# Final normalisation of the first block moved into the projection that opens the second block

## The reference

```python
def rmsnorm(x, g):
    y = x * rsqrt(mean(x * x, axis=-1) + EPS)
    return y * g

# first block, last lines
x = x + g2 * ec_moe(h2, router_w, exp_w1, exp_w3, exp_w2)   # 16 experts, 128 tokens each
return rmsnorm(x, final_g)                                  # input x of the second block

# second block, layer 0, first lines
h  = rmsnorm(x,   norm_g) * (1 + scale)   + shift           # 1024 tokens
hc = rmsnorm(ctx, norm_g) * (1 + scale_c) + shift_c         # 256 context tokens
p, pc = h @ w_in, hc @ w_in                                 # v, q, k, a|b, gates: 3072 columns
...
x = x + gate * mixer_out(...)                               # needs the normalised x again
```

## Time and profile before

| | us |
|---|---|
| median of 3 runs | 4442.1 (4436.2 to 4445.48) |
| the profiled execution | 4435.2 |
| its span, first to last instruction | 4433.4 |
| PE busy | 3832.5 (86%) |
| mean granted TensorE clock | 0.936 |

### The profile page before, as it was taken

The page is one execution under the profiler, slowest core; times in us unless marked ns, Lnnn a source line. Parts: engine busy times, 40 slices in busy tenths (PEclk is TensorE's granted clock), DMA queues, the critical chain, the costliest instruction groups (busy, mean ns, idle before and its releaser), DMA issues. The chain is left out here.

```text
span 4433.4 us, 44583 instructions
## 1 busy us (share of the span) xinstructions
PE 3832.5 (86%) x17507; PEld 2913.7 (66%) x17507; DVE 2574.1 (58%) x2821; ACT 1937.4 (44%) x2599; POOL 694.5 (16%) x582
## 2 busy tenths in 40 slices
PE   7899787894678789999999999499978897997988
PEld 2788643344666238787778777478867676786756
DVE  6421265327976468888888888553166525523753
ACT  4511110015545227676777776533156315423641
POOL 0200023210002101111212111320012223201222
PEclk9999898996888889999999999799989999999999
DMA  6322315101104569999999998534141234334123
GB/s 243 131 93 97 112 48 189 34 33 64 41 19 163 215 248 367 370 371 371 371 372 367 374 370 308 194 105 128 68 176 42 98 114 143 119 114 182 52 69 121
DMA packets 393094, 786.41 MB, mean 177 GB/s; under 512 B 26198, under 2 KB 109281, under 8 KB 392498
## 3 DMA queue, kind: packets, MB, share of 16 engines
q1 hardware_dynamic: 376502, 731.92, 46.1%
q0 software_dynamic: 11456, 41.16, 2.9%
q10 hardware_dynamic: 4928, 10.49, 0.7%
HBM read 671.99 MB, written 111.51 MB: 177 GB/s over the span
## 5 line engine op out<-in xcount | busy, mean ns | idle before, releaser
L2486 DVE TENSOR_TENSOR moe_w_low<-moe_w_raw,moe_w_high 128x2048 fp32r<-128x2048 f32 x384 | 882.0, 2341 | 163.7 <-ACT moe_w_high L2439 163.1
L2439 ACT ACTIVATE moe_w_high<-moe_w_raw 128x2048 fp32r<-128x2048 f32 x384 | 715.0, 1913 | 303.0 <-DMA moe_w_raw<-in_exp_w 297.0
L172 PE MATMUL moe_bank<-moe_w_high,moe_xgT_high 128*128 128x512 f32 x1024 | 404.2, 395 | 16.8 <-DVE moe_w_low L2486 12.0
L174 PE MATMUL moe_bank<-moe_w_high,moe_xgT_low 128*128 128x512 f32 x1024 | 399.6, 390 | 0.0
L173 PE MATMUL moe_bank<-moe_w_low,moe_xgT_high 128*128 128x512 f32 x1024 | 399.3, 390 | 0.0
L2758 DVE TENSOR_REDUCE layer_att_nb<-layer_att_scores 128x1 f32<-128x1280 f32 (+1 forms) x144 | 197.2, 1370 | 139.0 <-PE layer_att_scores L2664 138.9
L172 PEld LDWEIGHTS moe_bank<-moe_w_high,moe_xgT_high 128*128 128x128 f32 x1024 | 192.6, 188 | 62.8 <-DVE moe_w_low L2486 16.5
L172 PE MATMUL layer_front_bank<-layer_front_w_high,layer_front_hT_high 128*128 128x512 f32 (+1 forms) x608 | 228.8, 376 | 0.0
L174 PE MATMUL layer_front_bank<-layer_front_w_high,layer_front_hT_low 128*128 128x512 f32 (+1 forms) x608 | 222.7, 366 | 0.0
L173 PE MATMUL layer_front_bank<-layer_front_w_low,layer_front_hT_high 128*128 128x512 f32 (+1 forms) x608 | 222.4, 366 | 0.0
L174 PEld LDWEIGHTS moe_bank<-moe_w_high,moe_xgT_low 128*128 128x128 f32 x1024 | 192.6, 188 | 40.8
(11 more groups left out here) (461 smaller groups left out, 8498.3 us busy)
## 6 DMA issues: line engine op xcount, KB each, us to landing
moe_w_raw<-in_exp_w SPq DMA_DIRECT2D x192, 2048.0 KB, 10.3
mods_raw<-in_ada_w SPq DMA_DIRECT2D x12, 2048.0 KB, 9.0
h_raw<-in_w_mod SPq DMA_DIRECT2D x12, 2048.0 KB, 8.1
layer_front_raw<-in_w_in SPq DMA_DIRECT2D x48, 512.0 KB, 6.2
front_raw<-in_w_in SPq DMA_DIRECT2D x32, 512.0 KB, 6.3
proj_t<-front_out SPq DMA_DIRECT2D x48, 256.0 KB, 2.0
k_high<-layer_front_stageda SPq DMA_DIRECT2D x20, 512.0 KB, 3.3
k_low<-layer_front_stagedb SPq DMA_DIRECT2D x20, 512.0 KB, 4.7
```

Source lines behind the costliest of these rows:

```text
L172: nc.tensor.matmul(out, lhs[0], rhs[0], start=start, stop=False)
L174: return nc.tensor.matmul(out, lhs[1], rhs[0], start=False, stop=stop)
L2439: nc.scalar.activation(hi, x, ACT.Copy).then_inc(high, 1)
L2486: nc.vector.tensor_tensor(lo, x, hi.bitcast(F32), ALU.subtract).then_inc(low, 1)
```

## The change

`stage_final_norm` is gone. Its work is done inside layer0_front, as a step ahead of each tile's own normalisation: `measure_first` on ACT, `rescale` on DVE, `keep` on POOL (the store to `x2`). The two context tiles, which need none of it, come first (`order`), so the front's first loads don't depend on the experts. The weights of its group 0 and the context tiles are loaded by SP at the end of `stage_moe`, into the experts' own ring of buffers, which stays allocated; the wait for the last indirect transfer moves from POOL to SP, ahead of the load of the first token tile. In all three fronts `hT.high` is no longer computed a second time from PSUM but copied once from `whole`, as one 128 x 512 instruction on each of ACT and DVE, behind a wait for the piece before.

```diff
-def stage_front(core, name, segs, groups, rope=None):
+def stage_front(core, name, segs, order, groups, rope=None, space=None):
...
+    FIRST = NC_ if space else n
...
+        if space:
+            raw, out, x, junk, x2 = space.raw, space.out, space.x, space.junk, space.y
...
                 def load_x(t):
                     if t >= RX:
                         sp.wait_ge(turned, 2 * (t - RX) + 2)
+                    if t == FIRST:
+                        sp.wait_ge(core.scattered, 16 * E)
                     sp.dma_start(x[t % RX][:, :], tiles[t][0]).then_inc(core.load[t % RX].sem, 16)
...
+                if space:
+                    sp.dma_start(gain1, io["final_g"].partition_broadcast(P)).then_inc(gain1_loaded, 16)
...
+                if space:
+                    load_x(2)
+                    load_x(3)
...
+                def keep(t):
+                    pool.wait_ge(rescaled, t - FIRST + 1)
+                    pool.dma_start(core.x2[(t - FIRST) * P:(t - FIRST + 1) * P, :], x2[t % 2]).then_inc(core.store[t % 2].sem, 16)
+
                 for i in range(-2, N + 4):
                     if 0 <= i + 2 < n:
                         low_of(i + 2)
+                    if rescaled_tile(i + 3):
+                        keep(i + 3)
                     if R and i == 2:
                         rotation()
...
+                def measure_first(t):
+                    act.wait_ge(core.load[t % RX].sem, core.load[t % RX].at(t // RX + 1))
+                    if rescaled_tile(t - 2):
+                        act.wait_ge(core.store[t % 2].sem, kept(t - 2))
+                    core.act(act, nc.scalar.activation(x2[t % 2], x[t % RX][:, :], ACT.Square, accum_out=ss1[:, t:t + 1]))
+                    nc.scalar.activation(rms1[:, t:t + 1], ss1[:, t:t + 1], ACT.Sqrt, bias=core.eps[:, 0:1],
+                                         scale=1.0 / D).then_inc(rooted1, 1)
...
                     for k in range(4):
-                        for to in (whole[t % 2][:, k, :], hT.high[:, k, t * P:(t + 1) * P]):
-                            last = nc.scalar.activation(to, bank[4 + 2 * (t % 2)][:, k * P:(k + 1) * P], ACT.Identity,
-                                                        bias=sh[:, k:k + 1], scale=sc[:, k:k + 1])
-                    last.then_inc(out_a, 1)
+                        last = nc.scalar.activation(whole[t % 2][:, k, :], bank[4 + 2 * (t % 2)][:, k * P:(k + 1) * P],
+                                                    ACT.Identity, bias=sh[:, k:k + 1], scale=sc[:, k:k + 1])
+                    core.act(act, last)
+                    nc.scalar.activation(hT.high[:, 0:4, at], whole[t % 2][:, 0:4, :], ACT.Copy).then_inc(out_a, 1)
...
                 for i in range(-3, N + 4):
-                    if 0 <= i + 3 < n:
+                    if 0 <= i + 3 < FIRST:
                         measure(i + 3)
...
                     if 0 <= i + 2 < n:
                         modulate(i + 2)
+                    if rescaled_tile(i + 3):
+                        measure(i + 3)
+                    if rescaled_tile(i + 4):
+                        measure_first(i + 4)
...
+                def rescale(t):
+                    dve.wait_ge(rooted1, t - FIRST + 1)
+                    step(nc.vector.reciprocal(rms1[:, t:t + 1], rms1[:, t:t + 1]))
+                    if t == FIRST:
+                        dve.wait_ge(gain1_loaded, 16)
+                    nc.vector.scalar_tensor_tensor(x2[t % 2], x[t % RX][:, :], rms1[:, t:t + 1], gain1,
+                                                   ALU.mult, ALU.mult).then_inc(rescaled, 1)
...
+                    if rescaled_tile(i + 3):
+                        normalise(i + 3)
+                    if rescaled_tile(i + 4):
+                        rescale(i + 4)
...
                 for n in range(RW, E * UNITS):
                     sp.wait_ge(low, 2 * (n - RW + 1))
                     load_piece(core, sp, raw, n)
+                for j, load in enumerate(follow):
+                    sp.wait_ge(low, 2 * (E * UNITS - RW + j + 1))
+                    load(sp)
...
                 scatter(E - 1)
-                pool.wait_ge(scattered, 16 * E)
...
-def stage_final_norm(core, name="final"):
...
+    order = [(t + NT) % (NT + NC_) for t in range(NT + NC_)]
```

More of the change, by code:

```diff
@@ L618, in stage_front @@
         final[g] = i
-    assert [j[:2] for j in groups[0][1]] == [("tok", t) for t in range(n)]
+    assert [j[:2] for j in groups[0][1]] == [("tok", t) for t in order]
     plain = [i for i, (_, j) in enumerate(jobs) if j[0] != "rope"]
@@ L735, in low_of @@
                         c = slice(4 * half, 4 * half + 4)
-                        hi, lo = (v[:, c, t * P:(t + 1) * P] for v in (hT.high, hT.low))
+                        hi, lo = (v[:, c, tiles[t][3]] for v in (hT.high, hT.low))
                         nc.gpsimd.tensor_tensor(lo, whole[t % 2][:, c, :], hi.bitcast(F32), ALU.subtract).then_inc(split, 1)
@@ L947, in modulate @@
                     for k in range(4, 8):
-                        for to in (whole[t % 2][:, k, :], hT.high[:, k, t * P:(t + 1) * P]):
-                            last = nc.vector.tensor_scalar(to, bank[5 + 2 * (t % 2)][:, (k - 4) * P:(k - 3) * P],
-                                                           sc[:, k:k + 1], sh[:, k:k + 1], ALU.mult, ALU.add)
-                    last.then_inc(out_v, 1)
+                        last = nc.vector.tensor_scalar(whole[t % 2][:, k, :], bank[5 + 2 * (t % 2)][:, (k - 4) * P:(k - 3) * P],
+                                                       sc[:, k:k + 1], sh[:, k:k + 1], ALU.mult, ALU.add)
+                    step(last)
+                    nc.vector.tensor_copy(hT.high[:, 4:8, at], whole[t % 2][:, 4:8, :]).then_inc(out_v, 1)
                 def split_low(g, k):
@@ L1018, in stage_front @@
             core.hstore[RS + j].close(stores_of(j, R))
+        if space:
+            for j in range(2):
+                core.store[j].close(NT // 2)
 def stage_filter(core, name="filter"):
@@ L3273, in run_moe, with weights, context, __init__ @@
             late.close()
-        stage_moe(core, raw)
-    stage_final_norm(core)
-def run_second(core, out, l):
+        space = FrontSpace(raw, yo)
+        w = core.io["w_in_2"][0][:, 3 * BANK:4 * BANK]
+        def weights(sp):
+            for p in range(4):
+                load_front_weights(core, sp, space.raw, w, p)
+        def context(sp):
+            for t in range(NC_):
+                sp.dma_start(space.x[t], core.io["ctx_2"][0][t * P:(t + 1) * P, :]).then_inc(core.load[t].sem, 16)
+        stage_moe(core, raw, yo, (weights, context))
+        run_second_front(core, 0, space)
+class FrontSpace:
+    def __init__(self, raw, yo):
+        parts = lambda b, n: [b[:, i * (KD * BANK // n):(i + 1) * (KD * BANK // n)] for i in range(n)]
+        self.raw = raw[0][:, :].rearrange("p (k n) -> p k n", n=BANK)
+        self.x = parts(raw[1], 4)
+        self.out = parts(raw[2], 8)[0:6]
+        self.junk = parts(raw[2], 4)[3]
+        self.y = [b[:, :] for b in yo]
+def load_front_weights(core, sp, raw, w, p):
+    c = slice(2 * p, 2 * p + 2)
+    sp.dma_start(raw[:, c, :], w[2 * p * P:(2 * p + 2) * P, :].rearrange("(k p) n -> p k n", p=P)
+                 ).then_inc(core.load[4 + p].sem, 16)
+def run_second_front(core, l, space=None):
     io = core.io
@@ L3293, in run_second @@
     spans = [(0, 512), (512, 512)] + ([(SEQ, CTX)] if nctx else [])
-    groups = [(w[:, 3 * BANK:4 * BANK], [("tok", t, 0, BANK, core.v_tok[t * P:(t + 1) * P, :]) for t in range(NT + NC_)])]
+    order = [(t + NT) % (NT + NC_) for t in range(NT + NC_)]
+    groups = [(w[:, 3 * BANK:4 * BANK], [("tok", t, 0, BANK, core.v_tok[t * P:(t + 1) * P, :]) for t in order])]
     for i in range(2):
@@ L3304, in run_second @@
                         for s in range(4) for t0, n in spans]))
-    stage_front(core, name + "_front", [(x, core.sc[3 + 2 * l], m[:, 0:8, 0]), (ctx, core.sc[4 + 2 * l], m[:, 0:8, 1])],
-                groups, rope=io["qk_norm_g_2"][l])
+    segs = [(x, core.sc[3 + 2 * l], m[:, 0:8, 0], 0), (ctx, core.sc[4 + 2 * l], m[:, 0:8, 1], NT)]
+    stage_front(core, name + "_front", segs, order, groups, rope=io["qk_norm_g_2"][l], space=space)
+def run_second(core, out, l):
+    io = core.io
+    nctx = NC_ if l == 0 else 0
+    if l:
+        run_second_front(core, l)
+    x, ctx = (core.x2, io["ctx_2"][0]) if l == 0 else (core.x3, core.ctx3)
+    name = f"layer{l}"
+    tiles = range(NT + nctx)
     TL = NT + nctx
```

121 lines of the change are left out of this document (50 added, 71 removed).

## The result

The changed kernel takes 4408.5 us (median of 5 runs, 4401.08 to 4416.91), the kernel before, run beside it, 4439.25 (5 runs, 4434.14 to 4445.48): 30.75 us less, ratio 0.993 with a 95% interval of 0.9913 to 0.9947. The forecast was 4403, a gain of 38.9 us. The profiled spans differ by 4433.4 - 4404.4 = 29.0 us.

The account below looks back on a forecast made before the run. The removed stage was taken as bound by transfers and latency, the front behind it by PE. Gains of 44.1 and 1.3 us less 6.5 given back made 38.9, from 4442.1 to 4403 us; range 4394 to 4420.

Parts of the forecast that it names:

- The 69 us without PE: Between the experts' last matmul and the front's first: 69 us without PE work, which the change was to shorten.
- The meeting: Engines meeting between experts and front: forecast at 2771.7, with POOL's drain 2.66 us long and following the scatter's issue.
- the meeting still waits for the scatter: Rival: POOL's drain would not end before its transfer lands; 4.8 us less gain, 4408.0 us, chance 0.09.
- The chain on ACT: From the meeting to transposes of tile 2, ACT the longest chain: forecast 16.9 us.
- Group 0: Front's tiles 2 to 9: 6.5 us given back, PE waiting 4.8 us at tile 8 and 1.65 at tile 9.
- the first distance: Transposes of tile 2 to those of tile 3: forecast 8.04 us, PE's clock being reduced after its rest.
- the forecast's picture: Group 0: tiles 6 and 7 absorbed, PE waiting 4.8 us at tile 8 for the store behind `rotation()`.
- Copying once: High part copied once: 0.65 us saved in each of the two other fronts, 1.3 us together (0 to 2).
- 2.0 for modulate: ACT's modulate of tile 0 ahead of tile 2: four pieces of 0.345 us and one copy, 2.0 us.
- the upper bound: Cost of the high-part copy on DVE, standing behind a POOL instruction: 0.4 to 1.7 us.
- The signs named: Profile signs: no 43 us PE gap, first matmul 24 to 26 us behind, late transposes at tiles 8 and 9.
- the window: From the experts' last scatter's issue to transposes of tile 9: forecast 73.85 us, 37.6 shorter than before.

Follow-up runs that it names:

- wait_back: Changed kernel with POOL again waiting for the last scatter at the end of the experts' stage, ahead of its drain: 4407.9 us in one run.
- late_scatter: Changed kernel with the last expert's scatter issued by POOL in the next stage, after a POOL wait for `yout`: 4406.3 us, ratio 0.9928.
- best: Changed kernel with token loads one iteration earlier, `rotation()` at iteration 7, last scatter issued first in the next stage without the `yout` wait: 4399.1 us, ratio 0.9913.
- both links out: Changed kernel with token loads one iteration earlier and `rotation()` moved from iteration 2 to 7 in that front: 4404.7 us, ratio 0.9918.
- the loads sooner: Changed kernel with SP issuing each token load one iteration earlier in the second block's first front, `rotation()` unmoved: 4413.1 us in one run.
- late_rotation: Changed kernel with only `rotation()` moved on POOL from iteration 2 to iteration 7 of that front: 4406.0 us in one run.

## Why the prediction was right, and where not

**The 69 us without PE.** Right: the stretch is the one that the change works on, and the one that shrank, to 29.7 us.

**The meeting.** Wrong by 3.45 us. I took POOL's drain as a length of its own, 2.66 us, and gave the rival "the meeting still waits for the scatter" a chance of 0.09. That rival is what happens: with its own transfer under way POOL's drain took 7.89, 7.70 and 7.63 us in three profiles of the kernel; with nothing under way 2.66 and 2.58 (wait_back, late_scatter). The scatter took 6.3 us to land, so the drain ends some 1.4 us after. It doesn't wait and then drain in full: the rival's 4.8 us were 3.45. Its time, 4408.0, is nearer to the measured 4408.5 than my 4403, but half a microsecond is luck where medians of one kernel differ by several. That the row of before showed a drain "exactly behind" the landing said nothing, since the code had made POOL wait there.

**The chain on ACT.** 18.2 instead of 16.9 us. ACT's own rows came as forecast:

```profile
2777.91 1.06 ACT L834 ACTIVATE moe_w_raw<-moe_w_raw 128x1024 f32<-128x1024 f32 x1 [19.08 <-PEq L140]
2779.07 1.28 ACT L835 ACT_TABLE_LOAD   x1
2780.37 0.29 ACT L835 ACTIVATE layer_front_rms<-layer_front_ss,eps 128x1 f32<-128x1 f32 x1
2781.93 4.26 ACT L856 ACTIVATE layer_front_w_high<-moe_w_raw 128x512 fp32r<-128x512 f32 x8
2788.15 1.04 ACT L823 ACTIVATE moe_w_yo<-moe_w_raw 128x1024 f32<-128x1024 f32 x1
2792.33 1.06 ACT L834 ACTIVATE moe_w_raw<-moe_w_yo 128x1024 f32<-128x1024 f32 x1 [0.66 <-DVE moe_w_yo L992]
```

What was missed is how long DVE's instructions take beside POOL's differences. Each of these two runs beside one of POOL's L762, which start at 2789.95 and 2794.11 and take 1.26 and 1.27:

```profile
2789.98 2.31 DVE L992 SCALAR_TENSOR_TENSOR moe_w_yo<-moe_w_raw,layer_front_rms,layer_front_stageda 128x1024 f32<-128x1024 f32 x1
2794.14 1.79 DVE L999 TENSOR_SCALAR moe_w_raw<-moe_w_yo,layer_front_rstd 128x1024 f32<-128x1024 f32 x1
```

I had priced L992 at 1.29 and L999 at its median, 1.08. L992 took 2.31 and ACT stood idle for 0.66 us behind it; L999 took 0.71 more. Together that is 1.37, the missing 1.3. In late_scatter and in best, where no POOL instruction stood beside its first use, the line that answers to L992 took 1.29. The root started 0.02 us behind the table load, as before: no drain shows there.

**Group 0.** The sum came out right, 6.5 us, by luck: what makes it up was wrong. I expected tiles 6 and 7 absorbed, 4.8 us at tile 8 behind the store and 1.65 at tile 9. PE in fact waited 3.79 us at tile 7, nothing at tile 8 and 0.29 at tile 9. Of the other 2.4 us 2.1 are clock, which no step of mine had; 0.3 are small differences at tiles 7 and 9. By stretches, tiles 2 to 3, 3 to 6, 6 to 7, 7 to 8:

```profile
2796.00:2804.50 8.50, 8.50 (x33) 7.15 (x34) 6.46 (x10) 4.81 (x11) 3.54 (x4) 0.74 0.28 112
2804.50:2823.50 19.00, 19.00 (x97) 15.96 (x96) 13.21 (x26) 13.69 (x31) 12.69 (x15) 1.00 0.67 236
2823.50:2833.80 10.30, 6.52 (x33) 5.19 (x31) 6.58 (x9) 6.06 (x13) 9.83 (x11) 1.00 0.45 162
2833.80:2841.80 8.00, 8.00 (x32) 6.60 (x33) 5.64 (x10) 4.97 (x12) 3.31 (x4) 0.79 0.60 209
```

Behind the wait of 3.79 us PE is granted 0.79 on the mean of 8 us: matmuls start 0.43 us apart at first, 1.2 GHz, and 0.23 apart from 2838.17 on, 2.4 GHz. That turns 6.36 us into 8.03, 1.67 more. With both links out, where the wait at tile 7 is only 1.07 us, the clock was 1.00 in the same place and the distance 6.52. The other 0.43 is the first distance, 8.47 at a clock of 0.74 instead of 8.04 at 0.78; it differs between profiles of one kernel too (8.04 and 7.86 before, 8.47, 8.49 and 8.76 after).

Why tile 7 was late is seen on SP, ACT, POOL and DVE ahead of it:

```profile
2816.93 1.99 POOL L767 MEMSET layer_front_stagedb<- 128x1024 f32 x2
2819.80 0.47 SPq L704 DMA_DIRECT2D moe_w_raw<-x  x1
2825.56 1.06 ACT L823 ACTIVATE moe_w_yo<-moe_w_raw 128x1024 f32<-128x1024 f32 x1 [4.21 <-DMA moe_w_raw<-x]
2826.16 3.55 POOL L762 TENSOR_TENSOR layer_front_hT_low<-layer_front_whole,layer_front_hT_high 128x512 fp32r<-128x512 f32 x2
2829.65 0.63 POOL L802 DMA_DIRECT2D x<-moe_w_yo  x1
2829.86 2.00 DVE L1010 CAST layer_front_hT_high<-layer_front_whole 128x512 fp32r<-128x512 f32 x1
2831.97 1.78 DVE L999 TENSOR_SCALAR moe_w_raw<-moe_w_yo,layer_front_rstd 128x1024 f32<-128x1024 f32 x1
2833.03 1.06 ACT L823 ACTIVATE moe_w_yo<-moe_w_raw 128x1024 f32<-128x1024 f32 x1 [2.09 <-DMA x<-moe_w_yo]
```

Its load went out at 2819.80, 1.4 us later than forecast once the 7.4 us by which all of group 0 is later are taken off (2811.0 + 7.4), and took 5.8 us, not 4.0. ACT measured it at 2825.56, and on DVE the CAST of the tile before and L999 took 2.00 and 1.78 us. By my estimate that makes some 1.7 of the 3.79 us: ACT's root was ready at 2830.95, and with DVE's shortest durations L999 would have ended near 2832.0 instead of 2833.75. The store of tile 6 went out where I had put it, behind `rotation()` and `low_of(5)`, but landed 3.4 us later, not 6.2; ACT waited 2.09 us for it at tile 8, and PE didn't, since tile 7 and the clock had moved it back already. With the loads sooner the forecast's picture appears: nothing much at tile 7, 3.86 us at tile 8. So the store behind `rotation()` was a true cause, but stood behind another. The transfers from 2765 to 2865 (KB each, median us to landing), and the spread of the stores among them:

```profile
moe_w_raw<-x SPq DMA_DIRECT2D x8, 512.0 KB, 6.1
x<-moe_w_yo POOLq DMA_DIRECT2D x8, 512.0 KB, 3.2
DMA to landing us min/median/max: 3.1/3.2/7.4
```

The 6.1 is a median over all eight token loads, and four of these stand at the front's start, in pairs (6.8 us). Those of tiles 6 to 9 took 4.9, 5.7, 3.7 and 3.9 us, against 3.5 to 4.9 before: only tile 7's was longer than any row. POOL's stores got shorter than those of the removed stage, but for that of tile 5: issued at 2816.22, beside 2 MB of weights for the next group, it took 7.4 us.

**Copying once.** Forecast 0.65 us in each of the two other fronts. The first block's front is 1.3 to 1.8 us shorter in the mean, more than forecast, with lengths that vary by 2.8 among fronts of the same code; in layer 1, where they vary by 3.0, nothing can be seen. In the front that changed most it is worth 1.25 us ahead of tile 2, which the forecast had inside its 2.0 for modulate. On DVE the copy costs what it meets; its row, and that of POOL's difference, which answers to the earlier trace rows (min/median/max in ns):

```profile
L1010 DVE CAST layer_front_hT_high<-layer_front_whole x20: 426/427/1998, 2789.1 to 3719.4; 128x512 fp32r<-128x512 f32 x20
L762 POOL TENSOR_TENSOR layer_front_hT_low<-layer_front_whole,layer_front_hT_high x40: 1255/1290/2297, 2788.3 to 3721.1; 128x512 fp32r<-128x512 f32 x40
```

Median 0.43 us, at most 2.00, 1.57 more, a little over one POOL instruction (1.29); the upper bound was 1.7, so it was 0.3 short. The Trainium skill (page "SBUF — State Buffer", section "Who interferes with whom") has DVE and GpSimd exclude each other for a whole instruction when a cast uses both ports, and has a DVE instruction with two SBUF inputs contend with GpSimd's reads. The trace agrees in kind, by the CAST and by L992, which took 1.03 us more beside a POOL instruction of 1.26. Its other half, that transfers issued by GpSimd wait for DVE, hardly shows: their issue rows are 0.63 to 0.74 us (0.53 to 0.63 in the removed stage), and the median store landed in 3.2.

**The signs named.** The 43 us without PE are gone, as forecast, and the table load stands in the first measure. Between the products there are 29.7 us, not 24 to 26. The drain was to start at 2768.9, behind the issue, and to last 2.7; it starts at 2769.8, with the issue, and lasts 7.9. A first matmul near 2795 was named as the sign of a late meeting, and it came: 2797.61, with the experts' last matmul 2.6 us later than before. Late transposes at tiles 8 and 9 only: wrong, tile 7 was the first. Nothing was to change behind group 0, and nothing did: from the first job to the front's end it is 378.4 us before and 384.9 after, 6.5 more, the 6.5 of group 0 alone.

## What to carry to other kernels

Here a stage's end cost POOL the whole flight of the last indirect transfer it had issued, whether or not the code waits (plain transfers were not tried): issue such a transfer on the other side of the meeting, where it has the next stage's start to hide in. When work moves into a loop whose bound engine had little over 1 us of cover a step, look at the latencies in series (load, store, the queue that issues them), not at busy time alone, and count the clock that PE loses behind a wait; taking one link out can show little or nothing until the next is out too. And weigh each piece of a change: of the 32.8 us of the window, the weights loaded under the experts were worth 1.45.

## What the runs showed of the hardware

- POOL's drain at the end of the experts: 2.58 to 2.66 us with none of its transfers under way, 7.6 to 7.9 with an indirect one issued 0.2 us into it, which takes 6.0 to 6.3 to land. (2.6 us is no constant: at the ends of other stages of the same trace the drain lasts 0.05 to 3.4.) In best it stands at 2708.9 and lasts 12.2 us, beside the last but one scatter, issued at 2709.13 and landed 10.7 us later: again it ends 1.3 us behind the landing. It was over long before the meeting.
- PE after a wait of 3.79 us: 0.79 of its clock in the next 8 us, 1.67 us lost beside the wait; after one of 2.59 us (late_rotation) the same, 0.79 and 8.03 us. After one of 1.07 us (both links out): 1.00, and 0.16 us more than the usual distance.
- DVE beside one POOL instruction of 1.27 us: CAST 128x512 0.43 and 2.00 us, TENSOR_SCALAR 128x1024 0.75 and 1.79, SCALAR_TENSOR_TENSOR 128x1024 1.28 and 2.31.
